# A routed-experts stage that gathers its rows by index: the first two heads ranked on their first tokens alone, the query products regrouped, and two small reorderings elsewhere

## The chip, the cores and the metric

The kernel runs on one core of one Trainium2 chip. The metric is the device time of one execution in microseconds; lower is better. All tensors are float32.

## The reference, cut to what matters

Two transformer blocks run on 512 tokens of width 1024. The first block mixes tokens (a gated convolution, a short gated convolution and a spatial gating unit), then sends every token through product-key experts, then adds a per-layer embedding. The second block has gated linear attention, latent attention and two SwiGLU layers. The part that the change is about is the experts:

```python
q1, q2 = q[..., : D_KEY // 2], q[..., D_KEY // 2:]        # q = nf @ w_q, 8 heads x 256
s1 = einsum("thd,hkd->thk", q1, sub_keys[:, 0]); s2 = ... # 128 keys on each side
v1, i1 = top_k(s1, 16); v2, i2 = top_k(s2, 16)
cand = v1[..., :, None] + v2[..., None, :]                # 16 x 16 pairs
vals, ci = top_k(cand, 16)                                # 16 experts a head and token
idx = e1 * 128 + e2; gates = softmax(vals)
act = gelu(einsum("td,tkd->tk", x, expert_u[idx])) * gates
out = einsum("tk,tkd->td", act, expert_v[idx])            # 16384 experts x 1024 in u and in v
```

So each token reads 8 x 16 rows of 4 KB from `expert_u` and as many from `expert_v`: 512 x 128 x 2 rows, 537 MB in all.

## The kernel before, in words

**Engines and roles.** One instruction stream is written by hand for each engine: SP issues the loads of the dense weights, POOL (GpSimd) issues the indirect gathers of expert rows (and in the second block splits weights into a high and a low part), TensorE (PE) multiplies, ScalarE (ACT) moves results out of PSUM and applies functions, VectorE (DVE) ranks and takes dot products. They meet by semaphores only, so the order of each stream is the order in the code.

**Dense weights.** They come in units of 1024 x 256 (1 MB) through a ring of two slots, `wring`. SP's `unit` (line 376 holds its wait) issues a unit as soon as PE has finished the unit two before it. In `before` SP waits, after the last unit of `w_in`, until every product with `w_in` is done; then it issues the load of the 1 MB of `sub_keys` into `work` (line 421) and then the four units of `w_out`. PE's first product with `w_out` is line 797; the products with single rows of `mixT` alternate with the last small steps of the convolution heads (lines 721 and 726).

**Units of expert work.** The 512 tokens are four groups of 128 (a token per partition); a *unit* n of 32 is one group (n // 8) and one head (n % 8). For a unit, 16 gathers fetch the u rows and 16 the v rows of 128 tokens each (512 KB a gather). POOL issues them at line 1277 in the order u(n+1, 0), v(n, 0), u(n+1, 1), v(n, 1), ... into a ring of 16 slots. A gather into a slot first waits until DVE (u) or PE (v) has used what was in it, and POOL goes on in order behind that wait.

**DVE.** `u_row(n, k)` (line 2191) is a dot product of gathered u rows with the group's tokens, which PE has turned into PSUM (`tokens`, line 872). Ranking a unit, `topk`, is twelve small steps (`rank_keys`, line 2086, to `index_picks`, line 2167) that read the scores of that head and end with the 16 indices. `topk(0)` and `topk(1)` run before any row; in unit n, the steps of unit n + 2 run one after each of rows 3 to 14. `coefs(n-1)` (line 2205) is issued after row 2 of unit n and waits for ACT's gelu of unit n - 1.

**ACT.** In unit n: the exponentials of unit n + 2's gates (`gate_exp`, line 1575), the gelu of unit n (`hidden`, line 1581), the 16 scaled identities of unit n (`diagonals`, line 1589), the evacuation of the scores of the head before (`sc_evac`, line 1569), and of the query products of head n + 4 (`wq_evac`, line 1561), which end only with unit n's last row.

**PE.** `v_row(n, k)` (line 884) multiplies a diagonal with gathered v rows, two products of 512 columns accumulated in PSUM. The queries of a head are `w_q` (1024 x 256) times all 512 tokens, 16 products of 512 columns (`wq_matmul`, line 849), and its scores are eight products of 128 columns (`scores_of`, line 863). Heads 0 to 3 (`WQ_FIRST`) run before the loop over the units; heads 4 to 7 run one product behind each v row of units 0 to 3, and their scores after the last row. The keys are turned by `turn_keys` (line 835). The 24 sums over partitions for the second block's modulation (`ada`, line 782) run just before, and DVE's `modulation(0)` reads them right after the norm (line 1862).

**The split products of the second block.** POOL's `split_run` makes for each weight unit a rounded part (line 1250) and a rest (line 1254), DVE makes the rest `n_lo` of the activations chunk by chunk (line 2281), and PE multiplies high by high (line 586), low weights (line 590) and low activations (line 594). PE waits for each chunk of `n_lo` in the first unit of a stage.

**A matmul of float32 data is two records in the trace**, so x4 on line 884 is one v row, x2 on line 849 one query product, x16 on line 863 the scores of one head.

Of the kernel before, what the change touches and what calls it, by code (L numbers as in the profile page):

```python
# [19 lines left out]
P = 128  # L20
EPS = 1e-6

T = 512
# [9 lines left out]
WQ_FIRST = 4  # L33
# [32 lines left out]
def loop(eng, trips, counts):  # L66
# [9 lines left out]
    for (c, per), s, o in zip(counts, starts, outer):  # L76
# [6 lines left out]
        "hn_cen hn_sq hn_var hn_log hn_std hn_scaled hn_norm a_norm sg_read yb_step yb_ready ada_step ada_used sg_done h_ready keys_t keysT_ready sc_done sc_ready hs_max cand_max gexp "  # L83
# [8 lines left out]
def build(nc, A, out):  # L92
    with ExitStack() as ctx:
# [126 lines left out]
        keysT = arena[:, 22528:22528 + 2 * HEADS * P].rearrange("p (a k) -> p a k", a=2 * HEADS)  # L220
# [4 lines left out]
        R = Region(22528 + 2 * HEADS * P)  # L225
        qT = R.take(4, T)
        acc_sb = R.take(D)
# [18 lines left out]
        coef = R.take(2, TOPK)  # L246

# [96 lines left out]
        marks = {}  # L344

# [13 lines left out]
        def _(e):  # L359
# [124 lines left out]
        def _(e):  # L484
# [114 lines left out]
            def split_linear(name, n, high, hi, lo, evac, ready=None, lands=None, after=None):  # L599

                settle()
                if name:
                    marks[name] = (st["u"], [l.at for l in landed])

# [170 lines left out]
            def ada(part, bank):  # L775
# [5 lines left out]
                for m in range(24):  # L781
                    mm = e.matmul(ps[:, bank, m:m + 1], asum[:, m * P:(m + 1) * P], ones[:, 0:1], start=True, stop=True)
                inc(mm, "ada_cols")
# [56 lines left out]
            ada(0, 5)  # L840
# [58 lines left out]
            for h in range(WQ_FIRST):  # L899
                w = slot(DC)  # L900
                for j in range(2):
                    for k in range(DC):
                        if h == 0 and j == 0:
                            fresh(k)
                        wq_matmul(w, j, k)
                scores_of(h)
                if h == 0:
                    turn_keys(2)
                    turn_keys(3)
                    need("mod_ready", 1)  # L910
                    tokens(0)
            need("keysT_ready", 4)
            for n in range(UNITS):
# [13 lines left out]
                if h < HEADS:  # L927
                    scores_of(h)
# [3 lines left out]
            need("ptok_in", 16)  # L932
            need("acc_added", TT)
# [87 lines left out]
            def ffn(layer):  # L1021
# [3 lines left out]
                parts = operand()  # L1025
                counts = [(landed[0], 16), (landed[1], 16), (w_hi, 2), (w_lo, 2)]
# [144 lines left out]
        def _(e):  # L1171
# [67 lines left out]
            def split_run(name, stretches, high, lands=None):  # L1239
# [4 lines left out]
                def split(q, kc, n=16):  # L1244
# [8 lines left out]
                    e.sem_inc(S["pool_step"], 1)  # L1253
# [80 lines left out]
        def _(e):  # L1334
# [263 lines left out]
            for h in range(WQ_FIRST):  # L1598
# [5 lines left out]
                if h % 2:  # L1604
                    gate_exp(h // 2)
# [886 lines left out]
```

## Time and profile before

| | us |
|---|---|
| median of 3 runs (lowest, highest) | 3158.8 (3157.95, 3161.41) |
| the profiled execution's own time | 3153.37 |
| its span, first to last instruction | 3151.7 |
| first gather issued, last gather issued | 247.15, 1603.0 |
| PE busy, DVE busy, POOL busy, ACT busy | 2730.5, 1417.1, 1869.7, 623.7 |
| granted TensorE clock, mean | 0.934 |

Times inside the execution are counted from the span's start. The profiled execution's own time is 1.7 us above its span, and 5.4 us below the median of the runs shown. The stage of the gathers takes 43% of the span.

### The profile page before, as it was taken

What the parts mean: (1) busy time and instruction counts of PE and PEld (TensorE: products, weight loads), DVE (VectorE), ACT (ScalarE), POOL (GpSimd) and SP (SyncE); (2) the same over time, 40 slices, a digit from 0 to 9 for tenths busy, and PEclk for the clock granted to TensorE, in tenths of its full rate; (3) what the DMA queues carried; (4) which work ended last, traced back from release to release, by engine and by line L of the source; (5) the groups of instructions that cost most, each with busy time, mean ns of one, the idle gap of its engine ahead of it and who ended that gap; (6) DMA issues with size and microseconds to landing.
All of it is one profiled execution on the core that took longest, in us unless ns stands there. A gap on an engine that the chain in (4) does not pass through costs nothing.

```text
span 3151.7 us, 26631 instructions
## 1 busy us (share of the span) xinstructions
PE 2730.5 (87%) x8805; PEld 1621.9 (51%) x8805; DVE 1417.1 (45%) x3069; ACT 623.7 (20%) x1276; POOL 1869.7 (59%) x1393
## 2 busy tenths in 40 slices
PE   8998998777777777777788899899999998899998
PEld 7644443332233232332233376678878644678877
DVE  6747466666666666666514402331110346221111
ACT  2212122221121121222121211421110223121101
POOL 5205667767776777677758890246555385355653
PEclk9999999989998999899999899899999998899999
DMA  6338999999999999999974351022322251122222
GB/s 197 107 107 317 386 370 382 409 398 409 409 409 388 409 409 409 394 409 409 409 262 161 102 166 54 14 80 93 104 92 97 59 183 45 54 75 98 93 92 82
DMA packets 302996, 720.39 MB, mean 229 GB/s; under 512 B 24821, under 2 KB 159907, under 8 KB 302899
## 3 DMA queue, kind: packets, MB, share of 16 engines
q0 software_dynamic: 157248, 574.69, 46.7%
q1 hardware_dynamic: 133170, 131.92, 12.9%
q10 hardware_dynamic: 12480, 12.58, 1.2%
q8 instruction: 49, 0.80, 0.1%
q14 instruction: 49, 0.39, 0.0%
HBM read 717.02 MB, written 2.10 MB: 228 GB/s over the span
## 4 chain that ended last, share of the span: by engine, by line
PE 60%; POOL 15%; DMA 10%; issue 8%; DVE 4%; ACT 2%; SPq 0%; POOLq 0%; DVEq 0%; ACTq 0%
PE ps L884 11%; PE ps L594 10%; PE ps L590 10%; PE ps L586 10%; POOL arena L1277 9%; DMA arena<-in_expert_u_dram,arena 7%; POOL work L1277 3%; PE ps L849 3%; PE ps L982 2%; PE ps L532 2%; PE ps L543 2%; PE ps L797 2%; POOL arena L1223 1%; POOL arena L1220 1%; PE ps L1078 1%
## 5 line engine op out<-in xcount | busy, mean ns | idle before, releaser
L884 PE MATMUL ps<-arena 128*128 128x512 f32 x1536 | 761.1, 641 | 251.8 <-ACT arena L1589 165.9
L884 PEld LDWEIGHTS ps<-arena 128*128 128x128 f32 x1536 | 303.3, 205 | 689.5 <-issue 556.4
L2191 DVE CUSTOM_DVE_ANT_0 arena<-arena,ps 128x1024 f32<-128x1024 f32 x384 | 467.6, 1219 | 303.7 <-DMA arena<-in_expert_u_dram,arena 294.8
L1277 POOL DMA_INDIRECT arena<-in_expert_v_dram,arena x384 | 360.6, 939 | 189.3 <-PE ps L884 95.1
L1277 POOL DMA_INDIRECT arena<-in_expert_u_dram,arena x384 | 362.8, 945 | 149.9 <-issue 99.4
L1250 POOL TENSOR_SCALAR whi_f<-wring 128x2048 fp32r<-128x2048 f32 (+1 forms) x60 | 125.4, 2090 | 316.9 <-DMA wring<-in_ffn_w_in_dram 192.5
L1254 POOL TENSOR_TENSOR wlo<-wring,whi_f 128x2048 fp32r<-128x2048 f32 (+1 forms) x60 | 302.7, 5044 | 11.1 <-POOL whi_f L1250 11.1
L884 PE MATMUL ps<-work,arena 128*128 128x512 f32 x512 | 240.6, 602 | 27.1 <-DMA work<-in_expert_v_dram,arena 26.9
L590 PE MATMUL ps<-n_hi,wlo 128*128 128x512 f32 x1024 | 259.2, 396 | 0.0
L590 PEld LDWEIGHTS ps<-n_hi,wlo 128*128 128x128 f32 x1024 | 195.3, 191 | 43.0 <-issue 1.1
L2374 DVE TENSOR_TENSOR arena<-ps,arena 128x512 f32 x44 | 30.4, 692 | 407.6 <-PE ps L594 407.6
L2191 DVE CUSTOM_DVE_ANT_0 work<-work,ps 128x1024 f32<-128x1024 f32 x128 | 156.1, 1219 | 95.5 <-DMA work<-in_expert_u_dram,arena 95.5
L1589 ACT ACTIVATE arena<-ident,arena 128x128 f32<-128x128 f32 x512 | 153.0, 387 | 209.9 <-DVE arena L2205 209.9
L594 PE MATMUL ps<-n_lo,whi_f 128*128 128x512 f32 x704 | 180.2, 396 | 3.6 <-DVE n_lo L2281 3.6
L884 PEld LDWEIGHTS ps<-work,arena 128*128 128x128 f32 x512 | 93.2, 190 | 166.7 <-issue 98.0
L586 PE MATMUL ps<-n_hi,whi_f 128*128 128x512 f32 x704 | 170.5, 395 | 6.0 <-ACT n_hi L1428 6.0
L1896 DVE SCALAR_TENSOR_TENSOR hT<-ps,mod,hT 128x512 f32<-128x512 f32 x32 | 24.0, 751 | 298.1 <-PE ps L594 298.1
L586 PEld LDWEIGHTS ps<-n_hi,whi_f 128*128 128x128 f32 x704 | 133.7, 191 | 36.8 <-issue 7.6
L594 PEld LDWEIGHTS ps<-n_lo,whi_f 128*128 128x128 f32 x704 | 133.7, 190 | 36.5 <-DVE n_lo L2281 9.2
L1223 POOL TENSOR_TENSOR arena<-arena 128x1024 f32<-128x1024 f32 x72 | 141.7, 1968 | 5.6
L1277 POOL DMA_INDIRECT work<-in_expert_v_dram,arena x128 | 120.8, 944 | 40.7 <-issue 33.2
L1277 POOL DMA_INDIRECT work<-in_expert_u_dram,arena x128 | 120.5, 942 | 40.2 <-issue 31.7
(308 smaller groups left out, 3692.6 us busy)
## 6 DMA issues: line engine op xcount, KB each, us to landing
wring<-in_ffn_w_in_dram SPq DMA_DIRECT2D x44, 1024.0 KB, 5.0
arena<-in_ada_w_dram POOLq DMA_DIRECT2D x36, 1024.0 KB, 5.9
wring<-in_ffn_w_out_dram SPq DMA_DIRECT2D x16, 1408.0 KB, 6.1
arena<-in_ada_w_dram ACTq DMA_DIRECT2D x12, 1024.0 KB, 6.0
wring<-in_gla_w_in_dram SPq DMA_DIRECT2D x12, 1024.0 KB, 5.3
wring<-in_w_in_dram SPq DMA_DIRECT2D x9, 1024.0 KB, 5.6
wring<-in_w_q_dram SPq DMA_DIRECT2D x8, 1024.0 KB, 10.4
arena<-in_expert_u_dram,arena POOLq DMA_INDIRECT x384, 9.9
```

What stands on the lines that cost most here:

```text
L532: mm = e.matmul(ps[:, b, :], w[:, k, j * P:(j + 1) * P], rhs(k), start=(k == 0), stop=(k == kc - 1))
L586: e.matmul(banks[j], wh[:, k, cols[j]], hi(k), start=(start and k == 0), stop=False)
L590: e.matmul(banks[j], wl[:, k, cols[j]], hi(k), start=False, stop=False)
L594: mm = e.matmul(banks[j], wh[:, k, cols[j]], lo(k), start=False, stop=(stop and k == kc - 1))
L849: mm = e.matmul(ps[:, j, :], w[:, k, j * P:(j + 1) * P], nrhs(k), start=(k == 0), stop=(k == DC - 1))
L884: mm = e.matmul(ps[:, 6 + q, :], diag[:, k, :], slot_of(s)[:, q * 512:(q + 1) * 512], start=(n % HEADS == 0 and k == 0), stop=last)
L1223: stage(e.tensor_tensor(w[:, 0:half, :], w[:, 0:half, :], w[:, half:2 * half, :], ALU.add))
L1250: e.tensor_scalar(hi, w, 1.0, 0.0, ALU.mult, ALU.add).then_inc(w_split.sem, 1)
L1254: e.tensor_tensor(wlo[:, q, 0:kc * UNIT], w, hi.bitcast(F32), ALU.subtract).then_inc(S["w_lo"], 1)
L1277: e.indirect_dma_start(slot_of(seq), None, table, bass.IndirectOffsetOnAxis(ap=idx_flat[:, n * TOPK + k:n * TOPK + k + 1], axis=0)).then_i ...
L1589: inc(e.activation(diag[:, k, :], ident[:], ACT.Copy, scale=coef[:, n % 2, k:k + 1]), "diag_ready")
L2191: inc(e.tensor_tensor_reduce(slot_of(s), slot_of(s), ps[:, 4:6, :].rearrange("p a k -> p (a k)"), 1.0, 0.0, ALU.mult, ALU.add, dots[:, n % ...
```

## The change

It has four parts.

1. **Way in.** PE multiplies head 0 and then head 1 for the first 128 tokens only (products of 128 columns), scores them in banks 6 and 7, and does the other 384 columns later; DVE ranks units 0 and 1 from these. The tokens of group 0 are turned between. `ada(0)` and `modulation(0)` leave the way in: the 24 sums go in thirds behind rows 4, 8 and 12 of unit 6, and `modulation(0)` behind row 1 of unit 8. `WQ_FIRST` becomes 3.
2. **Order of ranking.** No ranking step runs in unit 0. Unit 2 is ranked in rows 3 to 8 of unit 1, unit 3 in rows 0 to 5 of unit 2, units 4 to 7 in rows 8 to 15 of the unit two before, the others as before.
3. **Later heads.** Heads 3 to 7 run two query products behind each of rows 0 to 7 of units 0 to 4, the scores right after row 7, and ACT evacuates both within that unit.
4. **Elsewhere.** The first two units of `w_out` are issued ahead of the wait and of `sub_keys`; and in POOL's split of a stage's second weight unit the subtraction first waits until all chunks of the stage's first `n_lo` are there (stages `gla_out`, `ffn0`, `mla_in`, `ffn1`).

Buffers move in the arena (`keysT`, `qT`, `acc_sb`), without other effect on the order of work. POOL's `iota` waits for `h_ready` in place of `ada_cols`.

```diff
-WQ_FIRST = 4
+WQ_FIRST = 3
...
+        def ranked(n):
+            return {0: (), 1: (2,), 2: (3, 4)}.get(n, (n + AHEAD,) if n + AHEAD < UNITS else ())
+        def rank_row(m, step):
+            if m == 2:
+                return 3 + step // 2
+            if m == 3:
+                return step // 2
+            if m < HEADS:
+                return 8 + 2 * step // 3
+            return 3 + step
...
@@ SP
-            e.wait_ge(done.sem, done.at)
+            projected = done.at
+            for j in range(2):
+                unit(w_out, j * UNIT, DC)
+            e.wait_ge(done.sem, projected)
             e.dma_start(keys_in, IN["sub_keys"][0].rearrange("h s k d -> k (h s) d")).then_inc(S["keys_in"], 16)
-            units(w_out, 0, 4, DC)
+            units(w_out, 2 * UNIT, 2, DC)
...
@@ PE
-            ada(0, 5)
             turn_keys(0)
             turn_keys(1)
             settle()
...
-            for h in range(WQ_FIRST):
-                w = slot(DC)
...
+            w0 = slot(DC)
+            for k in range(DC):
+                fresh(k)
                 for j in range(2):
+                    mm = first_matmul(w0, j, j, k)
+            inc(mm, "q_first")
+            w1 = slot(DC)
+            for j in range(2):
+                for k in range(DC):
+                    mm = first_matmul(w1, 2 + j, j, k)
+                if j == 0:
+                    first_scores(0)
+            inc(mm, "q_first")
+            tokens(0)
+            first_scores(1)
+            rest_matmuls(w0, 0)
+            need("sc_first", 2)
+            turn_keys(2)
+            turn_keys(3)
+            rest_matmuls(w0, 1)
+            need("q_taken", 2)
+            rest_scores(0)
+            for j in range(2):
+                e.wait_ge(act.sem, act.value(1))
+                rest_matmuls(w1, j)
+            rest_scores(1)
+            w = slot(DC)
...
+            scores_of(2)
...
                 for k in range(TOPK):
                     v_row(n, k)
-                    if h < HEADS:
-                        wq_matmul(w, k // DC, k % DC)
+                    if h < HEADS and k < DC:
+                        for i in range(2 * k, 2 * k + 2):
+                            wq_matmul(w, i // DC, i % DC)
+                        if k == DC - 1:
+                            scores_of(h)
+                    if n == HEADS - 2 and k in (4, 8, 12):
+                        if k == 4:
+                            settle()
+                        ada(0, 0, 2 * k - 8, 2 * k)
...
@@ POOL
                     e.sem_inc(S["pool_step"], 1)
+                    if second and lows.get(name):
+                        e.wait_ge(S["nlo_ready"], lows[name])
                     e.tensor_tensor(wlo[:, q, 0:kc * UNIT], w, hi.bitcast(F32), ALU.subtract).then_inc(S["w_lo"], 1)
...
-            e.wait_ge(S["ada_cols"], 1)
+            e.wait_ge(S["h_ready"], 1)
...
@@ ACT
+            first_evac(0)
+            first_scores(0)
+            first_evac(1)
+            first_scores(1)
+            rest_evac(0, (0,))
+            keys_evac(2)
+            keys_evac(3)
+            rest_evac(0, (1,))
+            rest_scores(0)
+            rest_evac(1)
+            rest_scores(1)
+            wq_evac(2)
+            sc_evac(2)
+            gate_exp(0)
+            gate_exp(1)
             for n in range(UNITS):
-                if n + AHEAD < UNITS:
-                    gate_exp(n + AHEAD)
+                for m in ranked(n):
+                    gate_exp(m)
                 hidden(n)
                 diagonals(n)
+                h = WQ_FIRST + n
+                if h < HEADS:
+                    wq_evac(h)
+                    sc_evac(h)
                 if n and n % HEADS == 0:
                     sums(n // HEADS - 1)
-                h = WQ_FIRST + n
-                if WQ_FIRST < h <= HEADS:
-                    sc_evac(h - 1)
-                if h < HEADS:
-                    wq_evac(h)
...
@@ DVE
-            modulation(0, bank=5)
...
-                need("sc_ready", 2 * (n % HEADS) + n // HEADS // 2 + 1)
+                if n < 2:
+                    need("sc_first", n + 1)
+                else:
+                    need("sc_ready", 2 * (n % HEADS) + n // HEADS // 2 + 1)
...
                     u_row(n, k)
+                    if k == 1 and n == HEADS:
+                        modulation(0, bank=0)
...
+                    for m in ranked(n):
+                        for s in range(len(STEPS)):
+                            if rank_row(m, s) == k:
+                                STEPS[s](m)
```

The new helpers: `first_matmul` is a product with `nT[:, k, 0:P]` (128 columns), `first_scores(h)` two products of 128 columns, `rest_matmuls(w, j)` eight products with `nT[:, k, P:T]` (384 columns), `rest_scores(h)` the six scores that are left. On ACT each has one evacuation.

## Rows read from the trace of the kernel before

**Rows 1.** The page, the span in 40 slices: what the DMA engines moved.

```profile
GB/s 197 107 107 317 386 370 382 409 398 409 409 409 388 409 409 409 394 409 409 409 262 161 102 166 54 14 80 93 104 92 97 59 183 45 54 75 98 93 92 82
```

**Rows 2.** Busy time by stretch; PE, PEld, DVE, ACT, POOL, clock, DMA share, GB/s.

```profile
441.00:487.00 46.00, 43.49 (x112) 20.02 (x112) 26.01 (x72) 9.89 (x25) 30.05 (x32) 1.00 0.97 374
522.00:564.00 42.00, 31.93 (x64) 12.66 (x64) 27.32 (x71) 7.68 (x22) 31.77 (x34) 0.91 1.03 409
```

**Rows 3.** Timeline, PE, way in: start, length, instruction, [idle before and its releaser].

```profile
211.10 7.72 PE L782 MATMUL ps<-ones,arena 128*128 128x1 f32 x48
...
220.42 15.72 PE L849 MATMUL ps<-nT,wring 128*128 128x512 f32 x32
236.84 2.05 PE L863 MATMUL ps<-arena 128*128 128x128 f32 x16 [0.69 <-ACT arena L1561]
...
288.00 2.05 PE L863 MATMUL ps<-arena 128*128 128x128 f32 x16 [0.69 <-ACT arena L1561]
```

**Rows 4.** Timeline, DVE, way in: the norm, and the ranking of unit 0.

```profile
212.61 5.36 DVE L1862 SCALAR_TENSOR_TENSOR nT<-hT,par,ps 128x512 f32<-128x512 f32 x8 [3.38 <-ACT ps L1361]
...
238.76 0.49 DVE L2086 MAX8 arena<-arena 128x8 f32<-128x128 f32 x2 [19.45 <-ACT arena L1569]
...
246.68 0.17 DVE L2167 SCALAR_TENSOR_TENSOR arena<-arena 128x16 uint32<-128x16 f32 x1
```

**Rows 5.** Timeline, POOL: the first two gathers, and one after a stall.

```profile
247.15 1.20 POOL L1277 DMA_INDIRECT arena<-in_expert_u_dram,arena  x1 [28.10 <-DVE arena L2167]
248.65 0.97 POOL L1277 DMA_INDIRECT arena<-in_expert_u_dram,arena  x1 [0.30 <-issue]
...
489.57 0.94 POOL L1277 DMA_INDIRECT arena<-in_expert_v_dram,arena  x1 [5.42 <-PE ps L884]
```

**Rows 6.** Timeline, PE: first v rows of units 0, 1, 4 and 7, query products between.

```profile
298.91 3.75 PE L884 MATMUL ps<-arena 128*128 128x512 f32 x4 [8.85 <-ACT arena L1589]
...
346.98 3.65 PE L884 MATMUL ps<-arena 128*128 128x512 f32 x4 [2.06 <-ACT arena L1589]
350.46 1.02 PE L849 MATMUL ps<-nT,wring 128*128 128x512 f32 x2
351.32 1.88 PE L884 MATMUL ps<-arena 128*128 128x512 f32 x4
...
487.35 10.54 PE L884 MATMUL ps<-arena 128*128 128x512 f32 x24 [2.05 <-ACT arena L1589]
...
605.37 12.74 PE L884 MATMUL ps<-arena 128*128 128x512 f32 x24 [5.67 <-ACT arena L1589]
```

**Rows 7.** Timeline, ACT: the table load ahead of the gelu of unit 0.

```profile
291.29 1.28 ACT L1581 ACT_TABLE_LOAD   x1
```

**Rows 8.** Timeline, DVE, unit 5: the ranking of unit 7, first and last step.

```profile
492.10 0.49 DVE L2086 MAX8 arena<-arena 128x8 f32<-128x128 f32 x2 [4.19 <-ACT arena L1569]
...
511.81 0.17 DVE L2167 SCALAR_TENSOR_TENSOR arena<-arena 128x16 uint32<-128x16 f32 x1
```

**Rows 9.** DMA issues from 230 to 300 us: KB each, median us to landing.

```profile
wring<-in_w_q_dram SPq DMA_DIRECT2D x4, 1024.0 KB, 16.8
```

**Rows 10.** Timeline, PE: the last head step and the first product with w_out.

```profile
133.80 1.13 PE L721 MATMUL ps<-arena,row 128*128 128x512 f32 x2
142.21 5.34 PE L797 MATMUL ps<-arena,wring 128*128 128x512 f32 x8 [7.29 <-DMA wring<-in_w_out_dram]
```

**Rows 11.** The chain that ended last, 110 to 212 us: start, length, what.

```profile
133.63 8.44 DMA wring<-in_w_out_dram
```

**Rows 12.** All of line 2281: ns min/median/max, first and last start, form.

```profile
L2281 DVE SCALAR_TENSOR_TENSOR n_lo<-nT,mod,n_hi x24: 737/740/5061, 2091.1 to 2771.2; 128x512 fp32r<-128x512 f32 x24
```

**Rows 13.** Timeline, start of ffn0: DVE, POOL, then PE.

```profile
2091.14 9.49 DVE L2281 SCALAR_TENSOR_TENSOR n_lo<-nT,mod,n_hi 128x512 fp32r<-128x512 f32 x8
...
2090.86 4.59 POOL L1254 TENSOR_TENSOR wlo<-wring,whi_f 128x2048 fp32r<-128x2048 f32 x1 [0.18 <-POOL whi_f L1250]
...
2101.28 3.61 PE L590 MATMUL ps<-n_hi,wlo 128*128 128x512 f32 x8
...
2106.62 3.79 PE L586 MATMUL ps<-n_hi,whi_f 128*128 128x512 f32 x16
```

More of the change, by code:

```diff
@@ L773, in _, with ada @@
                     AFTER[u]()
-            def ada(part, bank):
+            def ada(part, bank, first=0, last=24):
                 if part:
@@ L780, in ada @@
                     need("ada_used", 12)
-                for m in range(24):
+                for m in range(first, last):
                     mm = e.matmul(ps[:, bank, m:m + 1], asum[:, m * P:(m + 1) * P], ones[:, 0:1], start=True, stop=True)
-                inc(mm, "ada_cols")
+                if last == 24:
+                    inc(mm, "ada_cols")
             def mixed(k):
@@ L898, in _, with first_matmul @@
             fresh = norm_chunks(1)
-            for h in range(WQ_FIRST):
-                w = slot(DC)
-                for j in range(2):
[L902 to L911, printed above, removed]
+            def first_matmul(w, bank, j, k):
+                return e.matmul(ps[:, bank, 0:P], w[:, k, j * P:(j + 1) * P], nT[:, k, 0:P], start=(k == 0), stop=(k == DC - 1))
@@ new lines, in first_scores, with rest_matmuls @@
+            def first_scores(h):
+                need("q_taken", h + 1)
+                need("keysT_ready", 2)
+                for s in range(2):
+                    mm = e.matmul(ps[:, 6 + h, s * P:(s + 1) * P], qT[:, 2 * h + s, 0:P], keysT[:, 2 * h + s, :],
+                                  start=True, stop=True)
+                inc(mm, "sc_first_t")
+            def rest_matmuls(w, j):
+                for k in range(DC):
+                    mm = e.matmul(ps[:, j, P:T], w[:, k, j * P:(j + 1) * P], nT[:, k, P:T], start=(k == 0), stop=(k == DC - 1))
+                inc(mm, "chunk_done")
+                act.add()
@@ new lines, in rest_scores @@
+            def rest_scores(h):
+                settle()
+                if h:
+                    need("sc_ready", 2 * h)
+                for b in range(2):
+                    for q in range(2 if b == 0 else 0, 4):
+                        t, s = 2 * b + q // 2, q % 2
+                        mm = e.matmul(ps[:, 2 + b, q * P:(q + 1) * P], qT[:, 2 * h + s, t * P:(t + 1) * P],
+                                      keysT[:, 2 * h + s, :], start=True, stop=True)
+                    inc(mm, "sc_done")
@@ new lines, in _ @@
+            rest_matmuls(w0, 0)
[10 more added lines that the diff above has]
+            w = slot(DC)
+            for j in range(2):
+                for k in range(DC):
+                    wq_matmul(w, j, k)
+            scores_of(2)
@@ L1596, in sums, with first_evac @@
                 inc(e.activation(acc_sb, ps[:, 6:8, :].rearrange("p a k -> p (a k)"), ACT.Copy), "acc_ready")
-            for h in range(WQ_FIRST):
-                wq_evac(h)
-                sc_evac(h)
-                if h == 0:
-                    keys_evac(2)
-                    keys_evac(3)
-                if h % 2:
-                    gate_exp(h // 2)
+            def first_evac(h):
+                need("q_first", h + 1)
+                inc(e.activation(qT[:, 2 * h:2 * h + 2, 0:P], ps[:, 2 * h:2 * h + 2, 0:P], ACT.Copy), "q_taken")
```

67 lines of the change are left out of this document (31 added, 36 removed).

## The prediction

> **What bounds the kernel now.** I read the page's 40 slices first. From the fourth to the twentieth the DMA engines move up to 409 GB/s, and nothing later comes near it [rows 1]. A gather is 128 rows of 4 KB, 524,288 bytes, so at 409 GB/s one costs 1.28 us, and a unit of 32 gathers 41.0 us. Then I read the stretches: at 522 to 564 us DMA stands at 409, but at 441 to 487 us, where heads are still being multiplied behind the v rows, it is 374, PE is busy for 43.5 of 46 us, and a unit takes 46 us [rows 2]. So the stage has two regimes. In units 0 to 3 the round through PE, ACT and DVE sets the pace, from unit 4 on the transfers do. A start that comes t us sooner is kept to the end only if the units between don't spend it, so I follow when POOL can issue each gather.
>
> All times in the next two parts are on the trace's clock, as if the stages ahead of the norm had not moved.
>
> **Way in.** Now the last query product waits behind the 24 sums (7.7 us) and a head with all 512 tokens (15.7 us); unit 0's ranking starts at 238.8 and the first gather is issued at 247.2, 8.4 us behind it [rows 3 to 5]. Afterwards the products follow the norm's chunks, which end at 218.0 [rows 4]. Eight 128x128 products (16 records) take 2.05 us, so 0.26 each [rows 3]. The last two end at 218.5; I add 1.5 us for PE's clock, as the first head now takes 15.7 us where 16 products of 0.86 take 13.8 [rows 3, 6]. Half of head 1 and two scores (2.6 us) and a move to DVE (1.0 us, by half of the 1.92 us between line 863 and line 2086 [rows 3, 4]) bring unit 0's ranking to 223.3 and the first gather to 231.7: 15.5 us sooner. Turning the tokens and `modulation(0)` cost nothing here; the second is under 1 us of DVE between u rows, the first 1 us of PE.
>
> But PE has more to do before the first v row. From 220.1: head 1's first part 4.1, two scores pairs 1.0, tokens 0.9, the 32 products of 384 columns at 0.65 (three quarters of 0.86) 20.6, keys 1.8, remaining scores 3.1, two waits for evacuation 1.7, head 2 13.8 and its wait 0.85: 268. Head 2's weights can only be asked for when head 0's last column is done (237) and land after 16.8 us among gathers [rows 9], some 1.5 us late; no one is behind them but PE. From the scores of the last head of this stretch to the first v row ACT must do two evacuations, two exponentials, the table load that ends at 292.6, the gelu and a diagonal: 5.9 us after 288.0 in the rows [rows 3, 7]. That is behind head 2 in ACT's new order too. So v row (0, 0) comes at **275**, against 298.9 [rows 6]: 24 us are won here. Unit 0 then takes 27.5 (eight rows of two v and two query products, 3.44 each [rows 6]), 0.85, 2.05 of scores and 13.8 for the other rows, and unit 1 starts at 320, against 347.0.
>
> **Where it goes again.** Unit m = 4 to 7 is ranked from row 8 of unit m - 2 on. Its scores come from PE's unit m - 3, behind row 7. That unit's first v row waits for `coefs`, which DVE issues after row 2 of unit m - 2. So DVE passes rows 3 to 8 and then stands until PE has done eight double rows. With S the start of PE's unit: 27.5 us of rows, 0.85 for the evacuation, 1.92 from the scores' start to DVE [rows 3, 4]: S + 30.3. Behind it on DVE are the ranking and seven u rows. Eleven u rows and the ranking take 19.9 us [rows 8], the ranking alone 8.1 [rows 4], so seven take 15.6; then three u rows of the next unit (3.3), coefficient and diagonal (1.1): the next unit starts at **S + 50.3**. PE's own work in a unit is 44.2, so it idles 6 us. After such a gap (5.7 us) six v rows take 12.74 us, after one of 2.05 us 10.54 [rows 6]: 2.2 more. Units 2 to 5 start at 370.3, then 52.5 apart at 422.8, 475.3 and 527.8. In the trace the units are 46 to 48 apart. POOL's v(5, 8), the first gather that waits for PE's unit 5, comes 4.4 us later (one v row and 2.2 of clock), at 532.2. Now the same point one unit earlier, v(4, 8), is issued at 489.6 [rows 5], and 32 gathers at the DMA pace make 530.6. From there on both kernels run at the transfers' pace. **Way in and heads: 2 us slower.**
>
> The 24 sums in unit 6 cost 7.7 us of PE [rows 3]. PE is busy 31.9 of 42 us in such a unit [rows 2], so I take 0; with no cover it would be 7.7. The moved buffers and the new wait of `iota` cost nothing: POOL has 28 us of waiting ahead of its first gather [rows 5].
>
> A sentence on a page by itself: the Trainium skill, "TensorE: Matmul & The Clock Gate", section "Back-to-back issue gap", gives about 81 ns for a pass of 128 columns in a stream with weight loads, where the row shows 128 ns; by it the first gather would come 1.5 us sooner, and no more.
>
> **w_out first.** PE is done with the head step at 134.9 and waits 7.29 us for the first `w_out` unit, whose eight records (four products) then take 5.34 instead of 3.4 us; they end at 147.6 [rows 6, 10]. The load is issued at 133.6, behind the wait for all of `w_in` and the keys' issue, and takes 8.4 [rows 11]. Moved ahead, unit 0 is there in time, and unit 1 is asked for where the keys are now, some 1 us sooner, at 132.6. It lands at 141, and the last two products end at 142 to 144. ACT, DVE and PE run one short chain from here, and the next two units of `w_out` follow from PE: **5 us** (3.3 to 6). The keys come 1 us later and are wanted at 211 [rows 3].
>
> **POOL's subtraction.** DVE's eight chunks of `n_lo` should take 8 x 0.67, 5.4 us, like the norm's [rows 4]. They take 9.49 at the start of ffn0, because one of them lasts up to 5.06 while POOL subtracts for 4.59 (median 0.74) [rows 12, 13]. PE's first column with `n_lo` ends at 2101.3; it could end at 2096.8. With the wait POOL subtracts from 2096.6 to 2101.2, and PE wants the result after 3.7 us of high products of the next unit, so at 2104: hidden by 3 us. The x24 of rows 12 are three such stages, so 13.5 us. The dribble also costs clock: the 16 records behind it take 5.3 us instead of 3.6 [rows 13], three times 1.7 if it all comes back; I take half. **16 us** (13.5 to 19). In `gla_out` nothing is blocked now: 0.
>
> The Trainium skill, "SBUF — State Buffer", section "🔬 SBUF: two separate sides", states that DVE and GpSimd share a port pair as an exclusive lock that the first holds for its whole instruction. The 5.06 us agree. It speaks against the gain too: the moved subtraction would then block what DVE does next, in `mla_in` the rotation angles, which PE does not want for some 10 us; by it the sum stays.
>
> **The sum.** 3158.8 + 2 - 5 - 16 = **3139.8**. It is made against the profiled execution (own time 3153.4, span 3151.7, 1.7 around it), 5.4 us under the median; I carry the difference over. The chip can tell 0.2% (6.3 us) from no change.
>
> **The rivals.**
> - *DVE does not stand* (the gap closes, say since gathers rather than scores arrive last). Then PE's 44.5 us a unit hold for units 0 to 4: 275 + 222.5 and 2.2 give v(5, 8) at 499.7, which the transfers (193 gathers and 6 MB of `w_q` from 232 on, 495) allow. 31 us sooner, 3107. For: the order of ranking looks laid out for it. Against: the wait reads straight off the order of both streams, and DVE waits in this way today (4.19) [rows 8]. 0.12.
> - *POOL's wait gives nothing*, if `n_lo` is slow for its own reasons. 3156, within 0.2%. Against: 737 ns at the least, 5061 at the most [rows 12]. 0.06.
> - *Slower: PE stays at the low clock after each gap.* The gap ahead of units 2 to 5 would leave half of the eight double rows at 1.2 GHz, 13.8 us more in each of four rounds: 55, so 3195. It decides from 5.3 us a round beyond my 2.2. For: unit 1 shows 1.7 us lost after a mere 2 us. Against: the clock is 1.00 in rows as dense as these [rows 2]. 0.05.
> - Mine: 0.74, its own range 3124 (no clock lost, 6 and 19 us) to 3152 (each round 3 us longer, 3.3 and 13.5). Left over: 0.03.
>
> **How the numbers follow.** The likeliest case gives 3140. The range takes its own and reaches to the first rival: 3107 to 3152. Faster: 0.74, 0.12 and some of the rest, 0.88. Same: 0.06. Slower: 0.06.
>
> **What would show it.** First gather 15 us sooner relative to the norm, and 20 on the span's clock. v row (0, 0) at about 270. DVE's line 2086 idle for some 15 to 20 us in each of units 2 to 5, released by ACT, and units 2 to 5 of PE 50 to 53 apart; a pace of 44 would prove me wrong by 30 us. Line 2281 with no instance over 1 us. PE's first line 797 at 135.

## The result, and the profile of the changed kernel

The changed kernel takes 3127.5 us (median of four runs, 3125.4 to 3133.9) beside 3160.1 us for the kernel before on the same chip: a ratio of 0.9901, 95% interval 0.9884 to 0.9918. That is 31 us less, between 26 and 37. The profiled execution has a span of 3126.7 us and an own time of 3128.3, so it is a typical one. The profiled execution of before (span 3151.7) lies nearly 7 us under that median, and so the two traces differ by only 25.0 us. What is read out of the traces below has to add up to 25, not to 31.

Page of the changed kernel, the granted clock and what the DMA engines moved in 40 slices of 78 us:

```profile
PEclk9999999989998999888899898899999998899999
GB/s 198 108 157 396 372 342 341 409 398 409 409 409 390 409 409 409 392 409 409 409 265 164 92 183 41 27 81 94 94 91 99 71 178 52 43 92 94 94 93 82
```

Beside [rows 1] the gathers begin earlier (the third slice holds 157 in place of 107), then slices six and seven sink to 342 and 341 where before had 370 and 382, and from the eighth on both kernels stand at 409. So the way in is sooner, the head units are slower, and the middle of the stage is what it was.

Timelines of DVE and POOL at the way in, start, length, instruction, [idle before and its releaser]:

```profile
203.48 5.36 DVE L1974 SCALAR_TENSOR_TENSOR nT<-hT,par,ps 128x512 f32<-128x512 f32 x8 [3.38 <-ACT ps L1440]
212.39 0.49 DVE L2200 MAX8 arena<-arena 128x8 f32<-128x128 f32 x2 [3.55 <-ACT arena L1685]
220.32 0.17 DVE L2281 SCALAR_TENSOR_TENSOR arena<-arena 128x16 uint32<-128x16 f32 x1
220.79 1.20 POOL L1356 DMA_INDIRECT arena<-in_expert_u_dram,arena  x1 [21.00 <-DVE arena L2281]
```

The norm begins 9.1 us sooner than in [rows 4], and the first gather follows it by 17.3 us in place of 34.5 [rows 4, 5]: 26.4 us sooner in all. PE, from there to the first v row:

```profile
204.38 7.01 PE L921 MATMUL ps<-nT,wring 128*128 128x128 f32 x48 [1.37 <-DVE nT L1974]
228.19 10.49 PE L935 MATMUL ps<-nT,wring 128*128 128x384 f32 x32
241.99 14.00 PE L868 MATMUL ps<-nT,wring 128*128 128x512 f32 x32 [1.13 <-DMA wring<-in_w_q_dram]
262.39 3.75 PE L903 MATMUL ps<-arena 128*128 128x512 f32 x4 [3.66 <-ACT arena L1668]
```

v row (0, 0) comes at 262.4 in place of 298.9 [rows 6]. Line 868 is head 2, and its weights land 1.1 us late (1.5 forecast). Then DVE, where it comes to the ranking of units 4 and 5 (in the rounds of units 2 and 3):

```profile
339.54 0.49 DVE L2200 MAX8 arena<-arena 128x8 f32<-128x128 f32 x2 [14.36 <-ACT arena L1648]
391.49 0.49 DVE L2200 MAX8 arena<-arena 128x8 f32<-128x128 f32 x2 [22.40 <-ACT arena L1648]
```

Line 1648 is ACT's copy of the scores. DVE stands for 14 and 22 us where it stood 4.2 [rows 8]; in the next two rounds, units 4 and 5, it stands for 20.6 and 23.0. What this costs is seen best in the unit starts. I read from POOL's timeline when the first v gather of each unit was issued. In brackets is the time to the next unit:

| unit | before | changed |
|---|---|---|
| 0 | 268.6 (55.0) | 242.4 (54.9) |
| 2 | 371.5 (47.6) | 341.8 (53.3) |
| 3 | 419.1 (44.8) | 395.1 (50.2) |
| 4 | 463.9 (45.8) | 445.3 (53.1) |
| 5 | 509.7 (39.9) | 498.4 (41.9) |
| 6 | 549.6 (40.0) | 540.2 (40.0) |
| 31 | 1584.3 | 1573.4 |

At unit 2 the changed kernel leads by 29.7 us, at unit 6 by 9.4, at unit 31 by 10.9. The 9.1 us from ahead of the norm are about all that is left. PE's own units 2 to 5 start at 359.4, 411.4, 462.9 and 516.0, and six v rows behind such a gap take 12.60 us, much as the 12.74 of [rows 6]:

```profile
516.01 12.60 PE L903 MATMUL ps<-arena 128*128 128x512 f32 x24 [5.91 <-ACT arena L1668]
```

Timeline of PE at the end of the token mixing, with the products of `w_out` (line 817), and one row of the second pair of loads:

```profile
136.11 1.88 PE L817 MATMUL ps<-arena,wring 128*128 128x512 f32 x4
139.08 1.98 PE L817 MATMUL ps<-arena,wring 128*128 128x512 f32 x4 [1.09 <-DMA wring<-in_w_out_dram]
171.04 27.73 PE L817 MATMUL ps<-arena,wring 128*128 128x512 f32 x64 [1.33 <-DMA wring<-in_w_out_dram]
```

The wait of 7.29 us [rows 10] is down to 1.09, and four records (two products) take 1.88 and 1.98 us, where eight behind the gap took 5.34. From 142 us to the end of these products the granted clock is 1.00; before had 0.91 from 142 to 161 us and 0.94 from 178 to 208. At the start of ffn0, DVE and POOL:

```profile
2083.36 5.39 DVE L2377 SCALAR_TENSOR_TENSOR n_lo<-nT,mod,n_hi 128x512 fp32r<-128x512 f32 x8
2088.83 4.61 POOL L1333 TENSOR_TENSOR wlo<-wring,whi_f 128x2048 fp32r<-128x2048 f32 x1 [5.94 <-DVE n_lo L2377]
```

Eight chunks take 5.39 us where they took 9.49, and POOL's subtraction follows them [rows 13]. It ends at 2093.4, and PE's first product with its result starts at 2096.4, so it is hidden.

### The profile page after: what moved, and what is told of

Read it like the earlier page. It is cut to its first block, busy times and chain, and to the rows that moved or that the text cites. A ratio compares the mean times of both kernels' runs of the same rounds, so it can differ in the third digit from the quotient of the medians.

```text
span 3126.7 us, 26746 instructions
## 1 busy us (share of the span) xinstructions
PE 2722.7 (87%) x8869; PEld 1626.8 (52%) x8869; DVE 1410.3 (45%) x3069; ACT 625.4 (20%) x1280; POOL 1872.5 (60%) x1393
## 4 chain that ended last, share of the span: by engine, by line
PE 48%; POOL 14%; DMA 10%; issue 6%; DVE 3%; ACT 2%; POOLq 0%; DVEq 0%; ACTq 0%
PE ps L603 9%; PE ps L611 9%; PE ps L607 9%; PE ps L903 8%; POOL arena L1356 8%; DMA arena<-in_expert_u_dram,arena 8%; POOL work L1356 3%; PE ps L1058 2%; PE ps L549 2%; PE ps L560 2%; POOL arena L1300 1%; POOL arena L1297 1%; PE ps L1155 1%; PE ps L1049 1%; DMA arena<-in_expert_v_dram,arena 1%
## 5 line engine op out<-in xcount | busy, mean ns | idle before, releaser
L903 PE MATMUL ps<-work,arena 128*128 128x512 f32 x512 | 238.8, 601 | 24.8 <-DMA work<-in_expert_v_dram,arena 24.8
## 6 DMA issues: line engine op xcount, KB each, us to landing
wring<-in_w_q_dram SPq DMA_DIRECT2D x8, 1024.0 KB, 10.9
```

Source lines behind the costliest of these rows:

```text
L903: mm = e.matmul(ps[:, 6 + q, :], diag[:, k, :], slot_of(s)[:, q * 512:(q + 1) * 512], start=(n % HEADS == 0 and k == 0), stop=last)
```

## The experiments

Twelve runs were made, in three groups of four on three chips; each group has its own runs of the kernel before. The changed kernel did not run in the first group (where before takes 3157.4 us), so differences from it there are taken from its 3127.5 us above. By the ratios to the kernel before they come out within 1.5 us of what is given.

**POOL's wait taken out.**

```diff
-                    if second and lows.get(name):
-                        e.wait_ge(S["nlo_ready"], lows[name])
```

> The changed kernel without POOL's wait for n_lo; all else as changed. If the wait is what took the 9.5 us of n_lo to 5.4, line 2281's operation goes back to one instance of 4 to 5 us in each of the three stages ffn0, mla_in and ffn1, and the kernel is 17 us slower than the changed one (6.3 + 4.5 + 6.4 by the stages of the two traces, half of it clock). Rival: the faster stages come from another place, and it is under 5 us slower.

3144.7 us, ratio 0.996 (0.9946 to 0.9974), 17.2 above the changed kernel, as expected. Groups by line and form, the three starts with modulation (first this kernel, then the changed one):

```profile
L2375 DVE SCALAR_TENSOR_TENSOR n_lo<-nT,mod,n_hi 128x512 fp32r<-128x512 f32 x24 | 28.7, 1264 | 0.1
```

```profile
L2377 DVE SCALAR_TENSOR_TENSOR n_lo<-nT,mod,n_hi 128x512 fp32r<-128x512 f32 x24 | 16.2, 746 | 0.1
```

One chunk in each of the three stages is slow again (5.07 us at the most; none is over 0.753 in the changed kernel). The wait is worth 17 us by itself: 12.5 of it is DVE's time. The other 4.7 are what is left over; the record shows in ffn0 where such time goes, the 16 records behind the chunks taking 5.3 us here and 3.6 in the changed kernel.

**w_out back behind the keys.**

```diff
-            projected = done.at
-            for j in range(2):
-                unit(w_out, j * UNIT, DC)
-            e.wait_ge(done.sem, projected)
+            e.wait_ge(done.sem, done.at)
...
-            units(w_out, 2 * UNIT, 2, DC)
+            units(w_out, 0, 4, DC)
```

> The changed kernel with w_out again behind the wait and the keys. By the two traces the norm comes 10 us later after the last w_in product, more than the 5 forecast, because the load of unit 1 took 6.5 us and PE kept its clock. Expected 8 to 10 us slower than the changed kernel. Rival: 5 us, as forecast, the rest being a chance of the clock; PE's line 797 products then show 5.3 us for the first eight records in both.

3139.0 us, ratio 0.9941 (0.9926 to 0.9955): 11.6 above the changed kernel. Its norm begins 7.9 us later (DVE's timeline):

```profile
211.40 5.36 DVE L1971 SCALAR_TENSOR_TENSOR nT<-hT,par,ps 128x512 f32<-128x512 f32 x8 [3.38 <-ACT ps L1437]
```

So 8 us are seen directly, and PE's first eight records take 5.6 us again; by the medians it is 2 us more than the 8 to 10 expected. The other 3 to 4 lie in units 0 and 1: they take 56.6 and 46.6 us where the changed kernel has 54.9 and 44.4, and from unit 2 on this kernel is some 12 us behind. In the way in the weights of head 2 land 2.06 us late (1.13 in the changed kernel), and its 32 records take 15.7 us (14.0). Why moving `w_out` matters there was not tried.

**The way in and the heads alone** (both edits above undone).

> The way in, the order of ranking and the later heads alone: w_out and POOL's wait as before. Forecast 2 us slower than before; the traces say 2 us faster from the norm to the end of the experts. Expected within 4 us of the kernel before. Rival: the part carries what the medians show beyond the traces (32.6 against 25.0), and it is 8 us or more faster.

3157.2 us, ratio 0.9997 (0.9987 to 1.0006), so by itself the part that gives the change its name gives nothing on this chip: between 4 us less and 2 us more than before. Its first gather is issued at 232.2 and unit 2 starts at 353.3, 18 us ahead of before; unit 6 starts at 551.8, 2 us behind it. The three parts by medians, 0 + 11.6 + 17.2, make the measured 31 within its interval.

**Ranking one unit ahead.** If DVE's stand eats the lead, the cure is to rank unit m later, in the rounds of unit m - 1, when its scores have long been there.

```diff
-            return {0: (), 1: (2,), 2: (3, 4)}.get(n, (n + AHEAD,) if n + AHEAD < UNITS else ())
+            return (n + 1,) if 0 < n < UNITS - 1 else ()
...
-            if m == 2:
-                return 3 + step // 2
...
-            return 3 + step
+            return 3 + step // 2
```

> The changed kernel with unit n+1 ranked in rows 3 to 8 of unit n, for all n, so that no ranking step reads scores that PE has yet to make. If DVE's stand at row 8 sets the pace of units 2 to 5 (50 to 53 us), the pace falls to PE's own 44.2 plus 1 to 2, PE's unit 5 starts at 487 to 495 in place of 516, and the kernel is 20 to 27 us faster than the changed one. Rival 1, the gathers or their latency set that pace: under 6 us faster. Rival 2: units from 8 on lose, because indices come only when POOL wants them: slower.

3102.7 us, ratio 0.9826 (0.9809 to 0.9844), 24.8 below the changed kernel and 55 below before. DVE's wait ahead of MAX8 is gone, and units 2 to 5 start at 340.2, 386.5, 431.3 and 476.2; PE's unit 5 starts at 488.2, as expected, and from unit 8 to unit 31 it takes 954 us where the changed kernel takes 953, so the later units lose nothing. The profiled execution took 3114.2 us, 11.5 above its median; its last gather is issued 23.1 us sooner than in the changed kernel's trace (1569.0 against 1592.1), which is most of the 24.8 of the medians, and the second block behind it takes some 8 us longer. Busy time by stretch (PE, PEld, DVE, ACT, POOL, clock, DMA share, GB/s), first of this kernel, then of the changed one, over the same 156 us:

```profile
342.00:498.00 156.00, 150.19 (x383) 68.14 (x382) 94.97 (x255) 37.58 (x96) 105.06 (x113) 1.00 0.98 379
```

```profile
342.00:498.00 156.00, 136.22 (x336) 61.74 (x335) 78.18 (x214) 30.87 (x77) 90.45 (x96) 0.93 0.92 337
```

With the stand PE has 336 records in the stretch at a granted clock of 0.93, without it 383 at 1.00. The page of this kernel shows slices six and seven at 379 and 390 GB/s:

```profile
GB/s 199 108 156 401 396 379 390 409 397 409 409 409 389 409 409 409 389 409 409 409 221 152 108 162 41 14 88 101 94 96 93 83 167 41 53 82 94 94 93 83
```

**The stand made longer: units 4 to 7 ranked from row 3.** This and the next three ran on a second chip, on which the kernel before takes 3283.7 us.

```diff
-                return 8 + 2 * step // 3
+                return 3 + step
```

> The change, but units 4 to 7 are ranked from row 3 of the unit two ahead (rows 3 to 14) where the change ranks from row 8. The scores of such a unit leave ACT behind row 7, so VectorE, which comes to row 3 about 18 us before row 8, has to stand longer. Theory (VectorE's stand at the ranking sets the pace of the head units): the wait ahead of MAX8, 14.4 us and then 22.4 us in the changed kernel, grows by about 12 to 16 us in units 2 to 5 and what it hid is given back only in part; the pace goes from 51.8 us to 57 or more, and the time is 15 to 30 us above the changed kernel, 3142 to 3157. Rival (the pace is set by PE or by the gathers, and VectorE's stand is slack): the pace stays at 51 to 52 us and the time within 4 us of the changed kernel's 3127.

3294.7 us, ratio 1.0055 (1.003 to 1.0081). The changed kernel itself did not run on this chip; the nearest to it there is the kernel with its sums in one block (below), 3274.0, so this is 21 us above. DVE, first two lines of this kernel, then one of the kernel with its sums in one block:

```profile
366.29 0.49 DVE L2200 MAX8 arena<-arena 128x8 f32<-128x128 f32 x2 [27.32 <-ACT arena L1648]
426.66 0.49 DVE L2200 MAX8 arena<-arena 128x8 f32<-128x128 f32 x2 [31.04 <-ACT arena L1648]
```

```profile
423.22 0.49 DVE L2199 MAX8 arena<-arena 128x8 f32<-128x128 f32 x2 [24.27 <-ACT arena L1647]
```

Beside that kernel the stands grow by 11 and 7 us (16.75 to 27.32, 24.27 to 31.04), and units 2 to 4 take 59.0, 58.4 and 60.6 us in place of 56.7, 50.7 and 51.7. The forecast of 57 or more holds: where in the unit DVE stands, and with it how many of its rows are left behind the stand, sets the pace.

**Four query products behind each of rows 0 to 3**, the scores behind row 3. It ran here and, again, on the third chip below.

```diff
-                    if h < HEADS and k < DC:
-                        for i in range(2 * k, 2 * k + 2):
+                    if h < HEADS and k < DC // 2:
+                        for i in range(4 * k, 4 * k + 4):
...
-                        if k == DC - 1:
+                        if k == DC // 2 - 1:
```

> The change, but with four query products behind each of rows 0 to 3 of a head unit in place of two behind each of rows 0 to 7; the scores follow row 3. Ranking is still two units ahead, at row 8. Theory (VectorE waits at row 8 for scores that leave PE after row 7): the scores come some 12 us sooner, the wait of 22.4 us ahead of MAX8 falls to 10 us or less, the pace falls from 51.8 us to 45 to 47 us, and the time is 18 to 25 us below the changed kernel, 3102 to 3110. Rival (the products of a row now hold up the v rows of rows 0 to 3, and the gathers of the next unit wait for those slots): the pace stays above 50 us and the time within 5 us of 3127.

3277.8 us, ratio 0.9978 (0.9959 to 0.9996), 4 us above the kernel with its sums in one block: a miss for the expectation. DVE's stands do fall, to 12.0 and 9.2 us, but units 2 to 4 still take 50.9, 49.2 and 49.7 us. The run after the next shows why.

**The 24 sums in one block behind row 4.**

```diff
-                    if n == HEADS - 2 and k in (4, 8, 12):
-                        if k == 4:
-                            settle()
-                        ada(0, 0, 2 * k - 8, 2 * k)
+                    if n == HEADS - 2 and k == 4:
+                        settle()
+                        ada(0, 0)
```

> The change, but the 24 sums of unit 6 (1.84 us for each eight in the changed kernel) stand in one block behind row 4 in place of three blocks behind rows 4, 8 and 12. Theory (they stand in PE's slack, as costed at nothing): within 3 us of the changed kernel's 3127. Rival (the block of 5.5 us delays the v rows behind it and with them the gathers): 3 to 6 us slower, 3130 to 3133.

3274.0 us, ratio 0.997 (0.9953 to 0.9986). The changed kernel has 0.9968 on the third chip, so across two chips the place of the sums is within the noise, as forecast.

**Both cures of the stand together.**

> Both cures of VectorE's stand together: units ranked one ahead (3102.7 us by itself) and four query products behind each of rows 0 to 3. Theory (each removes the same wait, so the second has nothing left to remove): within 4 us of 3102.7. Rival (PE's query products are a second bound of the head units, hidden till now): another 5 us or more less, below 3098.

3265.3 us, ratio 0.9949 (0.993 to 0.9967). One ahead by itself has 0.9924 (0.9899 to 0.995) on the third chip; the intervals overlap, so the comparison across chips decides nothing but that there was no further 5 us to be had.

Its trace answers the question of the run with four products alone. DVE does not stand at the ranking here, and yet units 2 to 4 take 51.3, 49.2 and 49.9 us, as with the stand. One gather of POOL and, behind it, one row of DVE in unit 2:

```profile
421.30 0.94 POOL L1350 DMA_INDIRECT arena<-in_expert_v_dram,arena  x1 [5.71 <-PE ps L897]
```

```profile
428.10 1.22 DVE L2299 CUSTOM_DVE_ANT_0 arena<-arena,ps 128x1024 f32<-128x1024 f32 x1 [6.86 <-DMA arena<-in_expert_u_dram,arena]
```

A v gather waits 5.7 us for a slot that PE frees only behind four query products and the scores, and DVE then waits 6.9 us for a u row. In unit 0 of the changed kernel on the third chip, with two products a row, the longest such wait of POOL is 4.0 us and most are 1.3. So the rival of that run is what held: the crowded first rows hold up the gathers, and the pace of 50 us has this second cause. It would also explain why the second cure added nothing to the first.

On the second chip the kernel nearest to the changed one had a ratio of 0.997, not 0.990. Why became the question for the last four, on a third chip, with a trace of each.

> The kernel before, unchanged, for its trace beside those of the next three on one chip. On the chip of the last four runs the flat part of the expert stage moves about 370 GB/s in place of 409 and the kernel before takes 3283.7 us; there, in each changed kernel, ACT stood some 36 us ahead of its copies of unit 1's later tokens (queries of PE long done), and the first v row came at 291 us in place of 262. Theory (the first gathers, issued earlier, fill the DMA engines while ACT's code or another small transfer is still to come, so the stand is new with the change): the kernel before shows no such stand, its first v row lies 60 us behind its first gather or less. Rival (the stand is this chip's own and both kernels have it): it shows a stand of 20 us or more of ACT between its first gather and its first v row.

3282.7 us; beside the 25 runs of the same kernel in the group, 1.0022 (1.0007 to 1.0037). An interval that leaves out 1 for a kernel against itself says that here differences under 0.3% are not to be read.

> The changed kernel, unchanged. On a chip with 409 GB/s in the flat part: 0.990 of the kernel before, as measured, and the first v row 42 us behind the first gather. On a chip with 370 GB/s: theory (the gathers' rate sets the pace there and most of the way-in's gain, not POOL's 17 us, is lost): 0.996 to 0.998, since the kernel with its sums in one block gave 0.997; rival (the way in costs nothing extra there): 0.990.

3266.6 us, ratio 0.9968 (0.9954 to 0.9982): 11 us less than before instead of 31. The number is the theory's, but its reason, the gathers' rate, is not what the table below shows.

> The changed kernel with four query products behind each of rows 0 to 3. On a chip with 409 GB/s: theory (VectorE's stand ahead of MAX8 sets the head units' pace) 18 to 25 us below the changed kernel, rival within 5 us of it. On a chip with 370 GB/s a unit's 32 gathers take some 45 us by themselves, so the same cure can give 3 us a unit at most: within 8 us of the changed kernel.

3275.1 us, ratio 1.0003 (0.9984 to 1.0022): 8.5 above the changed kernel, so no gain of 3 us a unit but a loss.

> Units ranked one ahead, by itself. On a chip with 409 GB/s: 25 us below the changed kernel again (3102.7 against 3127.5). On a chip with 370 GB/s: 5 to 15 us below the changed kernel, since with both cures the ratio to the kernel before was 0.9949 against 0.997.

3253.7 us, ratio 0.9924 (0.9899 to 0.995): 12.9 below the changed kernel, as expected for such a chip.

The unit starts on the third chip, read as above:

| unit | before | changed | four products | one ahead |
|---|---|---|---|---|
| 0 | 272.8 (52.7) | 241.3 (84.9) | 241.6 (85.9) | 241.6 (85.6) |
| 1 | 325.5 (49.4) | 326.3 (45.8) | 327.4 (57.5) | 327.1 (45.0) |
| 2 | 374.9 (49.9) | 372.1 (55.5) | 384.9 (51.1) | 372.1 (49.5) |
| 3 | 424.8 (45.9) | 427.6 (51.8) | 436.0 (50.9) | 421.6 (45.8) |
| 4 | 470.7 (46.9) | 479.4 (52.2) | 486.9 (51.2) | 467.3 (45.9) |
| 6 | 564.4 (44.0) | 574.8 (47.0) | 581.4 (49.3) | 556.6 (46.6) |
| 31 | 1701.0 | 1714.9 | 1727.6 | 1701.8 |

On this chip the changed kernel's norm begins 12.8 us sooner than before's (202.4 against 215.2), its last gather is issued 14.1 us later (1738.1 against 1724.0): so there the way in and the heads cost some 27 us, where on the first chip they came out even. Neither loss is the gathers' rate: the lead of 31.5 us at unit 0 is gone at unit 1, and units 2 to 4 take 52 to 56 us where the transfers alone need 44 to 48. What comes behind the last gather takes 29 us less in these two traces (14 on the first chip).

Two things are in the table. The first is unit 0, 30 us longer in all three changed kernels than on the first chip (82 to 87 us in the four kernels on the second). ACT's timeline of the changed kernel on the third chip:

```profile
228.92 0.60 ACT L1701 ACTIVATE arena<-ps 128x512 f32<-128x512 f32 x1 [2.14 <-remote]
247.18 0.49 ACT L1692 ACTIVATE arena<-ps 128x384 f32<-128x384 f32 x1 [17.66 <-remote]
266.17 0.49 ACT L1692 ACTIVATE arena<-ps 128x384 f32<-128x384 f32 x1 [18.50 <-remote]
```

and PE's, of the same kernel:

```profile
227.09 10.49 PE L935 MATMUL ps<-nT,wring 128*128 128x384 f32 x32
266.71 2.93 PE L947 MATMUL ps<-arena 128*128 128x128 f32 x12 [29.13 <-ACT arena L1692]
291.29 3.75 PE L903 MATMUL ps<-arena 128*128 128x512 f32 x4 [3.66 <-ACT arena L1668]
```

PE had both products ready at 237.6, and ACT copies them at 247 and 266. "remote" is written where the profile finds no engine or queue of the kernel that released the wait. In the trace of the first chip the same two copies wait for PE alone (4.6 and 4.7 us). The kernel before, on the third chip, has the same kind of wait, shorter:

```profile
259.11 0.60 ACT L1569 ACTIVATE arena<-ps 128x512 f32<-128x512 f32 x1 [2.93 <-remote]
269.10 0.60 ACT L1561 ACTIVATE arena<-ps 128x512 f32<-128x512 f32 x1 [9.10 <-remote]
299.59 1.19 PE L884 MATMUL ps<-arena 128*128 128x512 f32 x1 [10.20 <-ACT arena L1589]
```

Its first v row lies 53.1 us behind its first gather, the changed kernel's 71.6. So the theory holds in its number (60 or less before) and the rival, 20 us or more in both, does not; but the waits aren't wholly new, they are 12 us in one kernel and 38 in the other. In both they fall into the time when gathers fill the DMA engines, which the change moved onto ACT's work for heads 0 and 1; but on the first chip the same overlap costs nothing. What ACT waits for isn't shown: its code coming through the DMA engines behind the gathers would fit, but the recorded packets of the instruction queues (one at 233 and the next at 278 us) do not end where its stands end. This stays open.

The second is the head units. One ahead shortens units 2 to 4 by 6.0 to 6.3 us each, here as on the first chip (5.4 to 8.2). Four products a row does shorten DVE's stand:

```profile
372.74 0.49 DVE L2200 MAX8 arena<-arena 128x8 f32<-128x128 f32 x2 [12.21 <-ACT arena L1648]
423.83 0.49 DVE L2200 MAX8 arena<-arena 128x8 f32<-128x128 f32 x2 [8.28 <-ACT arena L1648]
```

but the pace of units 3 and 4 falls only by 1 us, and unit 1 grows by 11.7. The expectation had mis-sized the gain: the sixteen products of a head take 13.8 us of PE wherever they stand, and only four v rows are no longer ahead of the scores, 6.9 us at most, not 12. DVE reaches row 8 later as well, since rows 0 to 3 come slower. In unit 1 PE idles 10.7 us ahead of its first v row and then never waits for a weight; ahead of that, in unit 0, POOL's v gather waits 5.71 us for PE and DVE 6.63 us for a u row, the pattern shown above.

## Why the prediction came out as it did

The direction and the range (3107 to 3152) held; the forecast of 3139.8 was 12 us too high. By its steps:

- **First gather.** 15.5 us sooner relative to the norm was forecast, 17.2 measured (34.5 to 17.3). The 1.5 us set aside for PE's clock was not needed: ACT copies head 0 at 209.6, 0.8 us behind the norm's last chunk. On the span's clock it is 26.4 where 20 was named, since `w_out` gave more.
- **v row (0, 0).** 275 on before's clock; less the 9.1 us of the norm that is 266, and 262.4 came. The 32 products of 384 columns took 21.2, as priced (20.6). Of the 3.5 us that are left 1.7 are those of the first gather; the rest has no single place.
- **DVE stands.** Right in place and nearly in size: released by ACT's copy of the scores, 14.4, 22.4, 20.6 and 23.0 us (15 to 20 forecast), PE's units 2 to 5 51.6 to 53.1 apart (52.5 forecast). The clock belongs to it: 0.93 over the stretch, and six v rows behind a gap take 12.60 us (12.74 in the rows, so 2.2 a round was right and the rival of a lasting low clock was not). Ranking one ahead shows the cost: 24.8 us, and the rival "DVE does not stand" had 31 us for the same state.
- **Way in and heads: 2 us slower.** From the norm to the end of the experts 1411.7 us before, 1410.0 after: 1.7 faster. By itself 0 (4 us less to 2 more). Right within 4 us, as the difference of a gain of some 20 and a loss of as much; and this is not luck, for both are right by themselves. On before's clock v(5, 8) was forecast at 532.2 and came at 529.1, and POOL still waits 2.0 us there for PE, as the working has it. That holds for the first chip only.
- **w_out first: 5 us, 3.3 to 6.** This is the term that was mis-sized. 9.1 us stand at the norm in the traces, 7.9 in the run with this edit alone undone, 11.6 in the medians. The second unit landed at 139 and not at 141, and the last two products ended at 141.1 where 142 to 144 was forecast: 6.5 us for the first pair in place of 3.6 to 5.6. The second pair had been put at nothing ("follow from PE") and gave 2.6: its wait is 0.9 us shorter, and its 64 records take 27.7 us in place of 29.4, at a granted clock of 1.00 in place of 0.94.
- **POOL's subtraction: 16 us.** 17.2 by the runs and 17.2 by the starts of `n_lo` in the traces of before and changed (the lead grows by 6.4 us over ffn0, 4.5 over mla and 6.4 over ffn1). DVE's part is 12.5 (13.5 forecast), so that half of the lost clock comes back (2.6 us) was too low; 4.7 are left for it.
- **gla_out and the sums of unit 6: 0.** Held: `n_lo` of gla_out takes 4.9 us in both, and unit 6 takes 40.0 us in both.

Redone from its own terms, the range of the likeliest case is some 3125 to 3153 and not 3124 to 3152, and the low-clock rival would turn the gain into a loss from 4.8 us a round (19 us in four), not from 5.3. Neither changes a chance. The 0.2% taken for no change is about the interval measured here, 0.17% to either side.

The Trainium skill, "SBUF — State Buffer", section "🔬 SBUF: two separate sides", has the port pair that DVE and GpSimd share as a lock that goes to one of them for a whole instruction; for DVE it names operations in a two-port mode and, against a GpSimd operation that reads SBUF, those with two SBUF inputs. The moved subtraction agrees in mla_in, where DVE's angle operation now lasts as long as POOL's subtraction (it took 0.49 before), and PE does not wait for it:

```profile
2465.85 4.75 DVE L2500 TENSOR_SCALAR arena<-arena,par 128x512 f32<-128x512 f32 x1
```

```profile
2465.56 4.75 POOL L1333 TENSOR_TENSOR wlo<-wring,whi_m 128x2048 fp32r<-128x2048 f32 x1 [5.59 <-DVE n_lo L2377]
```

Of the 12 us, 3 to 7 are w_out, 1 is POOL, 2 to 4 are the way in, and the rest is within the interval of the medians. All three lie on the same side, so the number is off by their sum. In the traces there is also a loss, in code that the change leaves alone: 3.1 us between the gated layer's start and ffn0.

## What to carry to other kernels

Starting a pipeline earlier pays only up to the first engine that must wait for something whose time did not move: ask for each later unit whether its inputs moved too, here the scores two units ahead. Two small edits beside the headline gave all of the gain on the first chip, and each was a wait whose full price is the wait plus the clock that PE loses behind it. When a gain of 20 us and a loss of 20 us cancel, the place of the loss is the next edit: ranking one unit ahead took the kernel to 3102.7 us. A second cure has to be looked at by itself too: four products a row shortened the stand, but made the gathers wait, and the pace stayed.

## What the runs showed of the hardware that was not expected

- **Chips differ more than the change.** The kernel before takes 3157 us on the first chip, 3284 and 3277 on the other two. A unit in the flat part of the stage mostly takes 40 to 42 us on the first and 44 to 48 on the others, and the gathers move 350 to 378 GB/s where they moved 409. The page of the changed kernel on the third chip:

```profile
GB/s 197 103 200 254 368 316 341 352 351 375 364 370 378 365 366 373 373 370 362 377 373 238 156 109 149 52 26 90 93 100 89 82 143 105 26 88 93 100 92 79
```

- **The same change is worth 31 us on one chip and 11 on another** (26 to 37, and 6 to 15). There unit 0 of the changed kernel is 30 us longer, with ACT's waits of 17.7 and 18.5 us in it; what they wait for stays open.
- **The clock falls in a stretch that the change doesn't touch.** In the gated layer the granted clock is 0.89 where it was 0.93, for the same code. Busy time by stretch, columns as above (changed, then before):

```profile
1882.00:1977.08 95.08, 93.86 (x384) 57.97 (x384) 22.49 (x14) 13.57 (x16) 1.44 (x2) 0.89 0.14 45
```

```profile
1893.00:1984.96 91.96, 90.51 (x385) 56.28 (x385) 22.48 (x14) 13.70 (x16) 1.27 (x2) 0.93 0.15 46
```

The same work, shifted by 11 us at its start, takes 3.1 us longer. Why the clock was lower was not tried.
